# Norm sum of a group in one split and two products, its chain one slot later

## What is computed

```
y = y_fwd + y_bwd + xs * d_skip            # (S, 8 groups, 256 channels)
y = y.reshape(b, S, SSM_W) * silu(z)
y = rms_norm(y.reshape(b, S, 8, 256), norm_g.reshape(8, 256))

def rms_norm(x, g):
    return x * rsqrt(mean(x * x, axis=-1) + EPS) * g
```

## Time and profile before

| | |
|---|---|
| median of 3 runs | 1528.83 us (1527.34 to 1530.46) |
| profiled execution, its own time | 1527.57 us |
| its span, first to last instruction | 1525.8 us |
| TensorE busy | 1514.9 us, 99% |
| VectorE busy | 963.9 us, 63% |
| ScalarE busy | 776.5 us, 51% |
| chain that ended last | TensorE 94%, VectorE 3%, DMA 2% |

### The profile page before, as it was taken

How to read it: one execution, slowest core, us unless ns; L and a number is a source line. 1 busy time by engine, 2 the same in 40 slices (tenths; PEclk the granted TensorE clock), 3 DMA queues, 4 the chain that set the end, 5 groups by cost and what they waited for, 6 DMA issues and landing times.

```text
span 1525.8 us, 21447 instructions
## 1 busy us (share of the span) xinstructions
PE 1514.9 (99%) x7564; PEld 1269.2 (83%) x7564; DVE 963.9 (63%) x1264; ACT 776.5 (51%) x1099; POOL 25.7 (2%) x36
## 2 busy tenths in 40 slices
PE   8999999999999999999999999999999999999999
PEld 7878888887888888888888888888888888888887
DVE  6988988878766666655554655455545456535643
ACT  6497777766645454544444443334433434334531
POOL 1000000000000000000000000000000000000000
PEclk9999999999999999999999999999999999999999
DMA  8766666685666656565566666666666666666664
GB/s 241 229 188 191 182 191 186 187 264 175 173 184 178 181 170 181 185 229 185 188 187 181 190 191 193 190 187 191 192 192 190 186 192 193 194 184 190 192 193 138
DMA packets 188233, 291.31 MB, mean 191 GB/s; under 512 B 13646, under 2 KB 69328, under 8 KB 188161
## 3 DMA queue, kind: packets, MB, share of 16 engines
q1 hardware_dynamic: 185424, 285.99, 62.4%
q10 hardware_dynamic: 2736, 4.30, 0.9%
HBM read 288.05 MB, written 5.34 MB: 192 GB/s over the span
## 4 chain that ended last, share of the span: by engine, by line
PE 94%; DVE 3%; DMA 2%; issue 1%; ACT 0%; SPq 0%; DVEq 0%
PE psum L1234 92%; DMA decay<-decay_rows 1%; DVE w_lo L807 1%; PE psum L1284 1%; DVE conv L847 1%; PE psum L1300 0%; PE psum L1363 0%; PE psum L1383 0%; DMA x_in<-in_x 0%; SPq L314 0%; DMA raw<-in_w_in 0%; PE psum L1310 0%; ACT w_hi L493 0%; DVE dt_p L1054 0%; DVE dt_r L1072 0%
## 5 line engine op out<-in xcount | busy, mean ns | idle before, releaser
L807 DVE TENSOR_TENSOR w_lo<-raw,w_hi 128x1024 fp32r<-128x1024 f32 x512 | 610.9, 1221 | 302.5 <-ACT w_hi L493 298.6
L493 ACT ACTIVATE w_hi<-raw 128x1024 fp32r<-128x1024 f32 x512 | 525.0, 1054 | 322.0 <-DMA raw<-in_w_down 155.3
L1234 PE MATMUL psum<-w_hi,actT 128*128 128x512 f32 x1536 | 497.8, 395 | 0.0
L1234 PEld LDWEIGHTS psum<-w_hi,actT 128*128 128x128 f32 x1536 | 288.4, 188 | 61.8 <-issue 3.0
L1234 PE MATMUL psum<-w_lo,actT 128*128 128x512 f32 x768 | 299.8, 390 | 0.0
L1234 PE MATMUL psum<-actT,w_hi 128*128 128x512 f32 x1024 | 256.6, 392 | 0.8 <-issue 0.8
L1234 PEld LDWEIGHTS psum<-actT,w_hi 128*128 128x128 f32 x1024 | 184.3, 189 | 34.7 <-issue 1.7
L1234 PE MATMUL psum<-w_hi,hid_lo 128*128 128x512 f32 x512 | 199.2, 389 | 0.0
L1234 PE MATMUL psum<-w_lo,hid_hi 128*128 128x512 f32 x512 | 199.2, 389 | 0.0
L1234 PE MATMUL psum<-w_hi,hid_hi 128*128 128x512 f32 x512 | 199.2, 389 | 0.0
L1234 PEld LDWEIGHTS psum<-w_lo,actT 128*128 128x128 f32 x768 | 144.4, 188 | 27.0
(11 more groups left out here) (197 smaller groups left out, 1050.1 us busy)
## 6 DMA issues: line engine op xcount, KB each, us to landing
raw<-in_w_in SPq DMA_DIRECT2D x128, 512.0 KB
raw<-in_w_up SPq DMA_DIRECT2D x128, 512.0 KB
raw<-in_w_down SPq DMA_DIRECT2D x128, 512.0 KB
raw<-in_w_out SPq DMA_DIRECT2D x64, 512.0 KB
raw<-in_w_in SPq DMA_DIRECT2D x64, 256.0 KB
raw<-in_w_in SPq DMA_DIRECT2D x128, 128.0 KB
decay<-decay_rows SPq DMA_DIRECT2D x14, 512.0 KB, 5.4
rel_tiles<-rel_rows ACTq DMA_DIRECT2D x1, 3072.0 KB, 23.6
```

The source lines that it names most:

```text
L493: act.activation(w_hi[j][:, :, :], raw[j][:, :, :], ACT.Copy).then_inc(hi_ready, 1)
L807: tt_(w_lo[j][:, :, :], raw[j][:, :, :], w_hi[j][:, :, :].bitcast(f32), ALU.subtract).then_inc(lo_dve, 1)
L1234: return pe.matmul(o, lhsT, rhs, start=first, stop=last, **kw)
```

## The change

The two channel tiles' squares are added on VectorE, in place in `gate_sq[:, 0]`, in slot k = 9. High and low part are made of the sum alone, 128x256, both in k = 10, and TensorE makes two products in k = 11 in place of four in k = 10. `mean_sq`, Ln and Exp go from k = 11 to 12, `group_norm` from 12 to 13, `cat_hi` from 13 to 14, `cat_lo` from 14 to 15. What belongs to the next group stays where it was. There is one new semaphore, `gate_summed`.

```
 ScalarE, ssd_slot
                     if k == 9:
                         act.wait_ge(gated, G + 2)
                         act.activation(gate_sq[:, :, :], gate[:, :, :], ACT.Square).then_inc(gate_squared, 1)
-                        act.wait_ge(gate_squared, G + 1)
-                        act.activation(sq_hi[:, :, :], gate_sq[:, :, :], ACT.Copy).then_inc(sq_high, 1)
-                    if k == 11:
+                    if k == 10:
+                        act.wait_ge(gate_summed, G + 1)
+                        act.activation(sq_hi[:, :], gate_sq[:, 0, :], ACT.Copy).then_inc(sq_high, 1)
+                    if k == 12:
                         act.wait_ge(m1_free, G + 2)
                         act.activation(log_ms[:, :], mean_sq[:, :], ACT.Ln).then_inc(ln_ready, 1)
...
-                    if k == 13:
+                    if k == 14:
                         act.wait_ge(normed, G + 1)
 VectorE, ssd_first and ssd_slot
-                if s - GROUP_SLOT[0] == 11:
+                if s - GROUP_SLOT[0] == 12:
                     group_mean(2 * m)
-                if s - GROUP_SLOT[1] == 11:
+                if s - GROUP_SLOT[1] == 12:
                     group_mean(2 * m + 1)
...
                     if k == 9:
+                        dve.wait_ge(gate_squared, G + 1)
+                        tt_(gate_sq[:, 0, :], gate_sq[:, 0, :], gate_sq[:, 1, :], ALU.add).then_inc(gate_summed, 1)
+                    if k == 10:
                         dve.wait_ge(sq_high, G + 1)
-                        tt_(sq_lo[:, :, :], gate_sq[:, :, :], sq_hi[:, :, :].bitcast(f32), ALU.subtract)\
+                        tt_(sq_lo[:, :], gate_sq[:, 0, :], sq_hi[:, :].bitcast(f32), ALU.subtract)\
                             .then_inc(sq_low, 1)
-                    if k == 12:
+                    if k == 13:
                         group_norm(G)
-                    if k == 14:
+                    if k == 15:
                         group_low(G)
 TensorE, ssd_slot
-                    if k == 10:
+                    if k == 11:
                         pe.wait_ge(sq_low, G + 1)
                         pe.wait_ge(ones_rounded, 1)
                         pe.wait_ge(cb_masked, G + 1)
-                        for c in range(2):
-                            mm(M1[:, 0:SEQ], ones_r[:, :], sq_lo[:, c, :], c == 0, False)
-                            ins = mm(M1[:, 0:SEQ], ones_r[:, :], sq_hi[:, c, :], False, c == 1)
-                        ins.then_inc(norm_summed, 1)
+                        mm(M1[:, 0:SEQ], ones_r[:, :], sq_lo[:, :], True, False)
+                        mm(M1[:, 0:SEQ], ones_r[:, :], sq_hi[:, :], False, True).then_inc(norm_summed, 1)
```

More of the change, by code:

```diff
@@ L177, in build @@
         newton = place("newton", [P, SEQ], at=at_of(lo2, 1024))
-        sq_hi = place("sq_hi", [P, 2, SEQ], f32r, at=cat_base + 32768)
-        sq_lo = place("sq_lo", [P, 2, SEQ], f32r, at=lo2[0] - 3072)
+        sq_hi = place("sq_hi", [P, SEQ], f32r, at=cat_base + 32768)
+        sq_lo = place("sq_lo", [P, SEQ], f32r, at=lo2[0] - 3072)
         gate_n = gate_t
@@ L286, in build @@
             "p_transposed", "pT_ready", "pv_done", "att_hi", "att_lo"))
+        gate_summed = sem("gate_summed")
         first_tile_done = sem("first_tile_done")
```

## The result

| | before | after |
|---|---|---|
| median of 7 runs, us | 1528.83 (1527.34 to 1530.48) | 1534.91 (1533.90 to 1535.99) |
| profiled execution, own time, us | 1527.57 | 1535.11 |
| its span, us | 1525.8 | 1533.4 |
| ratio of the times | | 1.0039, 95% interval 1.0029 to 1.0048 |

The account below looks back on a forecast made before the run. TensorE, busy 99% of the span, was taken as the bound. The terms -1.92 - 1.45 + 1.7 + 1.6 = -0.1 us gave 1527.5 against the profiled 1527.57, a median of 1528.7, range 1525.4 to 1533.0.

Parts of the forecast that it names:

- part 1: Norm products on TensorE: two of four, 0.12 us each, gone in each of 8 groups: -1.92 us.
- part 3: TensorE's wait for `sq_lo` in group 6 goes, as `rel_tiles` no longer stands ahead of the decay loads: -1.45 us.
- part 4: ScalarE's stretch from `mean_sq` through Ln, Exp and decays to `stage`: 6.04 us, about 0.5 us left before TensorE waits.
- (B): Rival: ScalarE's chain is longer than the rows say; with the first table load not hidden +4.7 us, 1533.5; chance 0.16.
- the margin of 0.5 us: Time between `stage` being ready and TensorE's turning transposes needing it, about 0.5 us; said to hold in the first window.
- part 5: VectorE comes 1.3 us late to `mean_sq`; TensorE waits for `stage` in the second and third windows: +1.7 us.
- 33.1 + 0.75 us: VectorE's work from the split behind Exp to the next `mean_sq`, 33.1 us, plus 0.75 us waiting for `w_hi`.
- part 6: Attention window, group 7: TensorE waits for `mix` of the second head, where there was no wait before: +1.6 us.
- Everything else is hidden: No further waits: splits of the main weights are ready four slots, 10.9 us, ahead of TensorE.

Follow-up runs that it names:

- e6: The kernel before with only `rel_tiles` issued in slot 2 of the attention window, behind group 7's decay loads: 1526.14 us, ratio 0.9985.
- e1: The changed kernel with 15 idle products at TensorE's start in place of 7: 1532.14 us, ratio 1.0025.
- e8: The changed kernel with 11 idle products in place of 7, the true replacement of the products gone ahead of the loop: 1530.78 us, ratio 1.0020.
- e9: The kernel before without its 7 idle products at the start (`IDLE = 0`): 1530.37 us, ratio 1.0015.
- e11: The kernel before with the sum in the old slots and `rel_tiles` issued in slot 2, 7 idle products, unpadded: 1527.03 us, ratio 0.9989.
- e3: The kernel before with only the one-slot move, still two splits and four norm products per group: 1528.69 us, ratio 1.0006.
- e5: The kernel before with only the sum and two norm products, in the old slots, 15 idle products: 1527.13 us, ratio 0.9994.
- e10: The changed kernel run again, unaltered, on another chip than its first measurement's or the same, beside the kernel before: 1533.14 us, ratio 1.0031.
- e4: The changed kernel with 15 idle products and the next group's last-head decays in k = 11, not 12: 1526.78 us, ratio 0.9993.
- e2: The kernel before with 15 idle products at the start in place of 7: 1529.25 us, ratio 1.0006.

## Why the prediction was wrong, point by point

**Products (its part 1): right.** In seven groups the chunk behind the products ends 0.24 us earlier, as forecast, in group 4 only 0.03: 1.7 us, not 1.9.

**The wait of 1.4 us (part 3): right.** ScalarE issues `rel_tiles` at 326.3 in place of 319.06, further back than the 4 us forecast, and the decay loads, issued at 324.9 and 325.4, go ahead of it: they land in 5.6 and 7.2 us, where they took up to 13.4. e6 shows the same cause alone. The forecast took its size from one execution, though, and other traces have waits of about 4 us there; that e6's median gained only 1.5 us all the same is not explained.

**The serial stretch (part 4): right in kind and size.** In the changed kernel's second window on ScalarE, to be held against the earlier trace rows:

```profile
194.79 1.28 ACT L565 ACT_TABLE_LOAD   x1
196.59 0.42 ACT L565 ACTIVATE log_ms<-mean_sq 128x256 f32<-128x256 f32 x1 [0.51 <-DVE mean_sq L878]
197.03 1.28 ACT L567 ACT_TABLE_LOAD   x1
198.32 0.42 ACT L567 ACTIVATE rnorm<-log_ms 128x256 f32<-128x256 f32 x1
198.65 1.26 ACT L532 ACTIVATE mix<-decay,tokn 128x128 f32<-128x128 f32 x4
...
200.92 1.24 ACT L507 ACTIVATE stage<-psum,small 128x512 f32<-128x512 f32 x2
```

The first load is over 0.51 us before Ln starts, so it is hidden, and rival (B) is out. From `mean_sq` at 196.14 to the end of `stage` at 202.16 are 6.02 us; the forecast was 6.04. Exp starts 1.29 us after its load, as before; the drain of which the Trainium skill speaks ("ScalarE: Activation LUTs", section "What ACT_TABLE_LOAD costs") shows in no row here either. In window 1 `stage` ends at 122.3 and TensorE turns it from 122.8 on, so the margin of 0.5 us held:

```profile
L1290 PE MATMUL psum<-ident,stage x8: 270/272/273, 122.8 to 123.6; 128*128 128x128 f32 x8
L507 ACT ACTIVATE stage<-psum,small x2: 668/670/672, 121.0 to 121.6; 128x512 f32<-128x512 f32 x2
```

**VectorE's lateness (part 5): right in kind, too small.** Forecast were two waits of 0.87 us, measured 1.39 and 1.63: +1.3 us in all. The step that was off is its start. It set `mean_sq` of group 1 at 0.44 behind the norm products, as if VectorE were on time there. VectorE in the changed kernel, and then the norm products of groups 1 and 2 on TensorE:

```profile
154.36 1.22 DVE L809 TENSOR_TENSOR w_lo<-raw,w_hi 128x1024 fp32r<-128x1024 f32 x1 [1.51 <-ACT w_hi L494]
...
156.64 0.42 DVE L878 TENSOR_SCALAR mean_sq<-psum 128x256 f32<-128x256 f32 x1
...
162.50 1.23 DVE L809 TENSOR_TENSOR w_lo<-raw,w_hi 128x1024 fp32r<-128x1024 f32 x1 [4.31 <-ACT w_hi L494]
...
196.14 0.42 DVE L878 TENSOR_SCALAR mean_sq<-psum 128x256 f32<-128x256 f32 x1
```

```profile
155.16 0.28 PE L1240 MATMUL psum<-sq_lo,ones_r 128*128 128x256 f32 x1
...
193.64 0.28 PE L1240 MATMUL psum<-sq_lo,ones_r 128*128 128x256 f32 x1
```

The norm products stand at 155.16, so `mean_sq` was due at 155.60 and came 1.04 us later: `mean_sq` now stands behind a split and `silu`, and that split had waited 1.51 us for its `w_hi`. The very effect that the prediction counted for group 2 (0.75 us) already works in group 1. The 5.86 us to the next split are as forecast (5.87), as is its idle of 4 to 6. From there on the forecast's 33.1 + 0.75 us lead to 196.35; measured is 196.14, and `mean_sq` is 2.06 us late against the products at 193.64. Less the margin of 0.5 this is the wait.

**The last group (part 6): right in kind, 0.5 us too small, for the same reason.** `mean_sq` comes 2.39 us late (355.99, products at 353.16), not 1.3 to 1.6. From the split behind Exp to the end of `mix` VectorE takes 11.45 us (forecast 11.58). The wait is 2.10, not 1.6. The half clock behind it, 1.7 us in some executions, was in no term.

**"Everything else is hidden": this is the step that failed.** It spoke of the splits, and those are hidden: no wait for `w_lo` stands in the changed kernel's SSD windows. But the sum took everything outside the SSD windows for unchanged, and there TensorE lost 3.6 us at the jump back of the MLP's loop. e1, e8, e9 and e11 show that it hangs on the place of TensorE's code, and that it has nothing to do with the new order. Without it the changed kernel is e8's, with a ratio of 1.0020, which on 1528.83 us would be 1531.9, inside the range: still slower, for the waits are 5.1 us, with the half clock behind them in that trace, against 3.2 us of gain.

In sum: forecast -0.1 against the profiled execution, measured +7.5. The difference: 3.6 from the loop, 1.7 from the half clock, 1.3 from part 5, 0.5 from part 6, 0.5 by which the chunks with the waits for `stage` grew beyond the waits, and 0.2 from the products, less 0.1 at the start. Of the rivals none was what happened. (B) gave 1533.5, nearest to the measured time, but by luck: its table load was hidden.

**Why the halves don't add up.** e3 (the move) came out at 1.0006, e5 (the sum) at 0.9994, both together (e1) at 1.0025. The waits for `stage` are 0.9 us in e3 and 3.0 in e1. Two products fewer in each group let TensorE ask 0.24 us earlier from group to group, 0.7 us after three groups, while VectorE's round, with the enforced idle in it, is no shorter (it even comes 0.45 us later, measured from the chunks ahead of group 0's norm products; what makes that is not shown). The two together are the 1.16 us by which the first wait differs, 1.39 and 0.23. In e3 `mean_sq` of group 2 stands 1.57 us behind the first norm product (196.88 and 195.31), of which 0.24 are the two more products; in the changed kernel 2.50 (196.14 and 193.64). Here the time taken from TensorE ahead of a wait on VectorE came back as a longer wait. That is worked out, not measured by itself.

**What stays open.** What in the place of the code makes the gaps. That one stands right at the jump back and the other at a fixed place of the code a few products behind it speaks for the fetching of instructions; no view shows that. Nor is it shown why the second gap is smaller in e9 (0.66 and 0.10 us) than in the changed kernel (1.40 and 1.35). Nor do I know why the half clock follows the 2.1 us wait in three traces (after, e1, e8) and not in a fourth (e10).

## What to carry to other kernels

When steps of a chain are merged into one slot, write down the whole serial stretch on the slower engine up to the next thing that the bound engine needs, and start with how late the engines already are there, not with the ideal time. Whoever removes instructions from the bound engine's program moves the code of every loop behind them: compare with a version padded to the old length before the new order is blamed or praised, and count the padding in the trace, not in the source: here one product of the source was two there. A large transfer that nobody needs soon belongs behind the small urgent ones; here that one move gave 1.5 us, nearly half of the best version's 3.1.

## What the hardware showed that I had not expected

- At the jump back of a loop on TensorE the gap was 0.3 to 0.8 us in nine kernels, and 1.7 to 2.1 us, in two pieces, in the changed kernel and e11, with the same body; e9 lay between (1.2 and 0.8). The second piece stood at the same place of the code, whether the loop lay 8 or 14 products earlier.
- A single wait of 2.1 us in an otherwise full TensorE was followed by 3.4 us at half clock in three traces, and by none in a fourth; waits of 1.2 to 1.6 us (e3, before, e4) by none; waits of 3.6 to 4.3 us by half clock each time, for 3.4 us (e2) and some 6.8 us (e5, e9). So the wait of 2.10 us cost 3.75 us in the changed kernel's trace, nearly twice its length.
